# Spreading the linear attention's norm factors over the rows: one fp32 product per head, or two fp32r products of a high and a low part

## The reference, cut to what matters

```
o_g = gla_chunked(q_g, k_g, v_g, log_a)                 # (1, 512 rows, 4 heads, 128)
o_g = rms_norm(o_g, gla_out_norm[i]).reshape(B, S, GLA_WIDTH) * jax.nn.silu(g_r)
...
h = h + jnp.concatenate([o_g, o_m], axis=-1) @ w_out[i]

def rms_norm(x, g):
    y = x * lax.rsqrt(jnp.mean(x * x, axis=-1, keepdims=True) + EPS)
    return y * g
```

## Time and profile before

| | |
|---|---|
| median of the runs | 1650.19 us |
| profiled execution, its own time | 1649.77 us |
| its span (first to last instruction) | 1648.0 us |
| TensorE busy with products | 1639.9 us |
| VectorE busy | 938.9 us |
| ScalarE busy | 615.4 us |
| GpSimd busy | 84.5 us |
| mean granted TensorE clock | 0.999 of full |

### The profile page before, as it was taken

The page is one execution under the profiler, slowest core; times in us unless marked ns, Lnnn a source line. Parts: engine busy times, 40 slices in busy tenths (PEclk is TensorE's granted clock), DMA queues, the critical chain, the costliest instruction groups (busy, mean ns, idle before and its releaser), DMA issues.

```text
span 1648.0 us, 19096 instructions
## 1 busy us (share of the span) xinstructions
PE 1639.9 (100%) x8084; PEld 1336.8 (81%) x8084; DVE 938.9 (57%) x1384; ACT 615.4 (37%) x828; POOL 84.5 (5%) x80
## 2 busy tenths in 40 slices
PE   9999999999999999999999999999999999999999
PEld 7877878888888888888888888877777888888887
DVE  6797675444343546577466457545655577366353
ACT  5576433332222336433223223455555333122121
POOL 1300000000000000000000000311201100000000
PEclk9999999999999999999999999999999999999999
DMA  5300227444453421222322222322221233222311
GB/s 195 116 26 27 103 77 131 132 87 110 100 119 83 123 103 52 77 103 102 128 77 102 103 83 96 126 77 92 85 76 52 77 103 103 102 102 93 109 60 71
DMA packets 27910, 155.94 MB, mean 95 GB/s; under 512 B 3696, under 2 KB 5120, under 8 KB 11952
## 3 DMA queue, kind: packets, MB, share of 16 engines
q1 hardware_dynamic: 26352, 149.84, 25.4%
q0 software_dynamic: 1328, 4.86, 5.1%
q10 hardware_dynamic: 144, 0.00, 0.0%
HBM read 149.98 MB, written 4.72 MB: 94 GB/s over the span
## 4 chain that ended last, share of the span: by engine, by line
PE 96%; DVE 2%; ACT 1%; POOL 0%; DMA 0%; issue 0%; SPq 0%; DVEq 0%
PE bank L584 26%; PE bank L586 26%; PE bank L585 26%; PE bank L590 3%; PE bank L592 3%; PE bank L591 3%; PE bank L1215 1%; PE bank L1225 1%; PE bank L1241 1%; PE bank L839 1%; PE bank L824 1%; PE bank L1101 0%; PE bank L1203 0%; PE bank L768 0%; PE bank L606 0%; PE bank L864 0%
## 5 line engine op out<-in xcount | busy, mean ns | idle before, releaser
L584 PE MATMUL bank<-AH,WH 128*128 128x512 f32 (+1 forms) x1150 | 451.4, 393 | 1.5 <-DVE gsil L2007 1.4
L586 PE MATMUL bank<-AH,WL 128*128 128x512 f32 (+1 forms) x1150 | 447.8, 389 | 0.0
L585 PE MATMUL bank<-AL,WH 128*128 128x512 f32 (+1 forms) x1150 | 447.6, 389 | 0.0
L1674 DVE TENSOR_TENSOR WL<-RAW,WH 128x2048 fp32r<-128x2048 f32 (+1 forms) x133 | 298.5, 2247 | 189.9 <-ACT WH L1286 189.9
L1286 ACT ACTIVATE WH<-RAW 128x2048 fp32r<-128x2048 f32 (+1 forms) x133 | 248.3, 1871 | 258.9 <-PE bank L586 240.3
L584 PEld LDWEIGHTS bank<-AH,WH 128*128 128x128 f32 (+1 forms) x1150 | 215.5, 187 | 49.9 <-issue 2.6
L586 PEld LDWEIGHTS bank<-AH,WL 128*128 128x128 f32 (+1 forms) x1150 | 215.5, 187 | 46.0
L585 PEld LDWEIGHTS bank<-AL,WH 128*128 128x128 f32 (+1 forms) x1150 | 215.5, 187 | 45.3 <-issue 1.0
L584 PE MATMUL bank<-HH,WH 128*128 128x512 f32 x608 | 239.6, 394 | 0.0
L586 PE MATMUL bank<-HH,WL 128*128 128x512 f32 x608 | 238.4, 392 | 0.0
L585 PE MATMUL bank<-HL,WH 128*128 128x512 f32 x608 | 236.0, 388 | 0.0
(11 more groups left out here) (305 smaller groups left out, 1733.1 us busy)
## 6 DMA issues: line engine op xcount, KB each, us to landing
RAW<-in_W SPq DMA_DIRECT2D x124, 1024.0 KB, 4.8
RAW<-in_W SPq DMA_DIRECT2D x9, 768.0 KB, 4.2
X<-in_XT SPq DMA_DIRECT2D x16, 256.0 KB, 5.3
ev_scratch<-ev POOLq DMA_DIRECT2D x16, 160.0 KB, 7.7
Gb<-ev_scratch SPq DMA_DIRECT2D x16, 128.0 KB, 3.2
out<-X SPq DMA_DIRECT2D x8, 256.0 KB, 2.0
Gb<-ev_scratch SPq DMA_DIRECT2D x16, 112.0 KB, 2.7
RAW<-in_W SPq DMA_DIRECT2D x2, 512.0 KB, 5.2
```

What stands on the lines that cost most here:

```text
L584: e.matmul(o, a, h, start=first, stop=False)
L585: e.matmul(o, a, l, start=False, stop=False)
L586: return e.matmul(o, c, h, start=False, stop=last)
L1674: e.tensor_tensor(k.WL[j][:, 0:n], k.RAW[RAW_OF[u]][:, 0:n], k.WH[j][:, 0:n].bitcast(F), SUB).then_inc(*WLO.mark(u))
```

## The change

DVE first makes the table of a head into a high part rh of type fp32r (L2074 of the new kernel) and the rest rl (L2076), then two diagonals from them, diagH and diagL, both fp32r. TensorE multiplies an fp32r block of ones, `onesr`, by one and then the other into the same bank. diagH lies over dg or rb as before, diagL over sq[0] or sq[1]. As sq holds the squares until the last row sums are taken, and rh and rl have one buffer each, there are new waits: for the row sums of head 3, and for the diagonal of the head before. `onesr` is copied once near the program's start.

```
+    k.onesr, k.rh, k.rl = a.tile("onesr", [P, P], R), a.tile("rh", [P, 4], R), a.tile("rl", [P, 4])
+    k.diagH = [a.over(f"diagH{i}", [P, 4, P], at, R) for i, at in enumerate((dg_at, rb_at))]
+    k.diagL = [a.over(f"diagL{i}", [P, 4, P], sq_at + 4 * S * i, R) for i in range(2)]
...
     def spread_out(h):
         w.wait_ge(DVE("odiag", h), *free[4 + h % 2])
-        e.matmul(bank[4 + h % 2][:, :], ones, (k.acc, k.rb)[h % 2][:, :], start=True, stop=True).then_inc(*MM.mark("ospread", h))
+        b = bank[4 + h % 2]
+        e.matmul(b[:, :], k.onesr[:, :], k.diagH[h % 2][:, :, :], start=True, stop=False)
+        e.matmul(b[:, :], k.onesr[:, :], k.diagL[h % 2][:, :, :], start=False, stop=True).then_inc(*MM.mark("ospread", h))
         free[4 + h % 2] = [DVE("gained", h)]
...
     w.wait_ge(arrived(k, "cst"))
+    e.tensor_copy(k.onesr[:, :], cst[:, C_ONE:C_ONE + P])
     spread_rows(0)
...
     def out_diagonal(h):
         w.wait_ge(POOL("rg", h // 2))
         if h > 1:
             w.wait_ge(MM("ospread", h - 2))
-        r = k.rg[:, 4 * h:4 * h + 4]
-        d = (dg[:, :, :], rb[:, :].rearrange("p (q n) -> p q n", n=P))[h % 2]
-        e.tensor_tensor(d, ident[:, None, :].to_broadcast([P, 4, P]), r[:, :, None].to_broadcast([P, 4, P]), MUL).then_inc(
-            *DVE.mark("odiag", h))
+        r, eye = k.rg[:, 4 * h:4 * h + 4], ident[:, None, :].to_broadcast([P, 4, P])
+        if h:
+            w.wait_ge(DVE("odiag", h - 1))
+        e.tensor_copy(k.rh[:, :], r).then_inc(*DVE.mark("orh", h))
+        w.wait_ge(DVE("orh", h), MM("osum", 3))
+        e.tensor_tensor(k.rl[:, :], r, k.rh[:, :].bitcast(F), SUB).then_inc(*DVE.mark("orl", h))
+        e.tensor_tensor(k.diagH[h % 2][:, :, :], eye, k.rh[:, :].bitcast(F)[:, :, None].to_broadcast([P, 4, P]), MUL)
+        w.wait_ge(DVE("orl", h))
+        e.tensor_tensor(k.diagL[h % 2][:, :, :], eye, k.rl[:, :, None].to_broadcast([P, 4, P]), MUL).then_inc(*DVE.mark("odiag", h))
```

More of the change, by code:

```diff
@@ L188, in memory @@
     k.WL = [a.tile(f"WL{i}", [P, UE], R) for i in range(NW)]
+    rb_at = a.at
     k.rb = a.tile("rb", [P, S])
+    sq_at = a.at
     k.sq = [a.tile(f"sq{i}", [P, S]) for i in range(2)]
```

## The result

The new kernel takes 1659.22 us (median of four runs, 1657.82 to 1659.61), the kernel before 1650.28 on the same chip (four runs, 1648.57 to 1650.54). The ratio is 1.0058 [1.0045, 1.007]: 8.9 us slower. The forecast was 1650.9, with 1652.6 as the upper end of its range, so it was wrong, and on the side to which it had given 0.04. The profiled execution's own time is 1659.61 us and its span 1657.8.

What follows compares the result with a forecast made beforehand. TensorE was taken as the bound, VectorE as late in 200 to 220 us: its second pair's extra 2.0 us less slack outweighs TensorE's 1.6 us saving, +0.71 us on the 1650.19 median, giving 1650.9 us, range 1649.0 to 1652.6.

Steps and rivals of the forecast that it cites:

- the side to which it had given 0.04: Whole kernel: measurably slower, beyond 0.2% or 3.3 us, from a clock fall and more behind it; chance 0.04.
- The step that the prediction worked out: Second pair of heads, 200 to 220 us: VectorE's extra 2.0 us less its slack delays TensorE by +0.71 us.
- 1.60 us a head: VectorE, per head: cast, subtraction, diagH and diagL take 1.60 us where one diagonal took 0.60.
- the means where they were forecast: VectorE, after the first pair's diagonals: the means start at 206.65 instead of 203.77.
- the forecast 0.6 and 1.1: TensorE waits 0.6 us for head 2's diagonal and about 1.1 us for head 3's before their spreads.
- the wait for X: TensorE waits 0.8 us before the second half's second output block, which starts near 219.95.
- Rival 2: 200 to 220 us: VectorE's additions come early enough, TensorE's whole 1.6 us saving stays, 1648.6 us; chance 0.06.
- Rival 4: Spreads on TensorE: fp32r products take 0.43 us, no saving, total +0.8 us; counted within the forecast's 0.68.
- rival 1: VectorE's heads: waits on its own results are free, 1.36 us a head, +0.1 us, 1650.3 us; chance 0.13.
- Rival 3: 213 to 224 us: new waits bring a second clock fall, 1.5 us on top, +2.2, 1652.4 us; chance 0.13.
- From 219.95 all is shifted alike, if nothing else slips: Everything behind the second half's second output block keeps its pace, only shifted by 0.7 us, with no further loss.
- The copy to `onesr`: VectorE near the program's start: one 128x128 operation fits where it waited 1.23 us for POOL, costing nothing.

Runs made afterwards that it cites:

- e2_tail: The new kernel with onesr, rh and rl in free memory behind all other tiles, which stand at their old places: 1650.9 us, ratio 1.0006.
- e1: The kernel before with 576 unused bytes behind m4, so later tiles move as in the new kernel, no instruction changed: 1657.01 us, ratio 1.0042.
- e3: The kernel before with 192 unused bytes behind m4: 1644.87 us, ratio 0.9969.
- e6: The kernel before with 320 unused bytes behind m4: 1656.96 us, ratio 1.0042.
- e7: The kernel before with 128 unused bytes behind m4: 1657.71 us, ratio 1.0047.
- e11: The kernel before with 224 unused bytes behind m4: 1657.43 us, ratio 1.0046.
- e12: The kernel before with 704 unused bytes behind m4: 1645.04 us, ratio 0.9973.
- e10_after_pad128: The new kernel with 128 unused bytes of padding: 1645.9 us, ratio 0.9979.
- e9_best: The new kernel with rh and rl made once for two heads, diagL formed by ScalarE, and 64 bytes of padding: 1643.49 us, ratio 0.9966.
- e4_pad448: The kernel before with 448 unused bytes behind m4: 1643.52 us, ratio 0.9961.
- e5_all64: The kernel before with every tile moved by 64 bytes: 1650.17 us, ratio 0.9998.
- e8_w64: The kernel before with weights WH and WL moved 64 bytes, activations AH, AL, HH and HL unmoved modulo 256: 1667.26 us, ratio 1.0103.

## Why the prediction was wrong

**What held.** The step that the prediction worked out was right in place and size: products of 0.23 us, 1.60 us a head, the means where they were forecast (207.51 less the older shift of 0.78 is 206.73, for 206.65), waits of 0.57 and 0.87 for the forecast 0.6 and 1.1, the wait for X (0.58, forecast 0.8), VectorE as the bound of the stretch. It cost +0.79 in the profiles and +0.95 by e2_tail's median, for a forecast of +0.71. Rival 2 (the saving stays) fell with the waits. Its slack of 1.1 us on VectorE was counted from three of the idle times in brackets; by the starts, twelve operations of 0.60 in the 8.98 us from 209.52 to 218.50 leave 1.8. The sum of +0.71 went by starts and isn't touched by that. Rival 4 (products of 0.43) fell with the spacing. The waits on VectorE's own results aren't free, so rival 1 fell too: in the new kernel diagL runs from 205.31 to the start of its waiter at 206.03, 0.72 us, and diagH, without a waiter, from 204.71 to 205.31, 0.60. The rule of the Trainium skill, "VectorE: DVE Perf Modes", "The DRAIN you can't avoid", by which the semaphore adds nothing, doesn't agree with that.

Rival 3 (a second fall of the clock) didn't come either. Two windows of the new kernel, the first as the earlier trace rows, the second over the new waits:

```profile
194.70:201.90 7.20, 7.20 (x30) 5.93 (x30) 3.88 (x5) 3.19 (x4) 1.64 (x1) 0.76 0.08 9
209.00:222.00 13.00, 10.98 (x45) 8.03 (x45) 11.65 (x20) 2.46 (x4) 0.39 (x1) 1.00 0.06 10
```

The granted clock there is 1.00.

**What failed.** The step "From 219.95 all is shifted alike, if nothing else slips". The prediction asked of the rest of the program only whether anything arrives late. The diff had one more effect, visible in its first line: three tiles declared ahead of HH and HL. It put the moving operand of 1824 products, a quarter of TensorE's time, from distance 64 to 128, at 4.3 ns each: 425.3 - 417.4 = 7.9 us, a term that the prediction had at nothing. The products with OH and OL, which also lie behind the three tiles, rise from about 229.5 to 233 ns, 173 distances, +0.6 us. Together 8.5 where the profiles show 8.27 behind the first HH product. The copy to `onesr` was priced as an instruction, at nothing, and the 576 bytes weren't priced at all. The form of the error is that the cost of TensorE's product was taken as one number for one shape, while the earlier trace rows already mixed operands: those eleven products, of 0.232, aren't of HH.

The Trainium skill's page "SBUF — State Buffer", section "Operand start alignment", would not have warned: it lets an fp32 operand start at any multiple of 4 bytes, and says itself that this is about legality and that nothing was timed. In these runs all places are legal and their times differ by 24 us.

**What stays open.** 0.78 us of the profiles' difference arises ahead of attended 4. Most of it is at the start, where the first product of L584 stands at 6.92 before and of L590 at 7.37 now, behind a transfer of X that landed at 5.79:

```profile
1.66 4.13 DMA X<-in_XT
...
7.37 0.45 PE bank L590
```

Before, the chain began with a weight transfer that landed at 4.70. No run ties it to the change: the kernels with the instructions of before and fast AH products (e1, e3 to e7, e11 and e12) reach attended 0 anywhere from 180.10 to 180.64 us, before at 179.99, the new kernel at 180.79, e2_tail and e10_after_pad128 at 180.67, and e9_best, which has the copy to `onesr` as well, at 180.15. Most of the 0.78 us can be the scatter of single executions; the rest stays open. Nor is it shown why the distance matters, why 256 is its period (0 and 256 modulo 512 were alike, and so were the two places of 128, by 320 and by 576; no shorter period fits 0, 32, 64, 128 and 192), or why 64 lies between and 32 doesn't. Which read of the weights counts, that of the same product or that of the next one's, can't be told, as all weights stand at one place modulo 256. Not shown either: whether it holds for products whose weights aren't loaded anew each time. All of these load them.

## What to carry to other kernels

A tile added to a memory plan is an edit to every instruction whose operands lie behind it: put new tiles last, or compare the places of all hot operands before and after. In a stream of fp32r products of 128x512 with a weight load each, keep the moving operand and the stationary one at the same place modulo 256 bytes; in this kernel one line of padding was worth 5.1 us (e4_pad448, 1643.53 against 1648.59 among executions at a granted clock of 1.000; the medians' 6.4 has luck with the clock in it), and the change that was meant to speed it up cost some 0.8 us with the places held. And when TensorE's busy time rises with an unchanged count and no idle time, compare the mean ns of its groups by operand before looking for waits.

## What the runs showed of the hardware

- In a stream of fp32r products of 128x512, the mean distance between starts is 226.7 ns where the moving operand stands 0 bytes behind the stationary one modulo 256, 229.0 ns at 64, and 233.3 ns at 32, 128 and 192; only these five were measured.
- Both operands moved together by 64 bytes cost nothing (e5_all64, 1650.17 against 1649.91 us), and which of the two is moved makes no difference (e8_w64).
- On VectorE, a 128x512 operation whose follower waits for its result takes 0.72 us from start to start, one without such a wait 0.60 (new kernel, 205.31 to 206.03 and 204.71 to 205.31).
- The clock's fall behind the narrow products comes in some profiled executions only, and it explains part of the scatter. Two windows over the same stretch, e4_pad448 without it:

```profile
192.00:206.00 14.00, 14.00 (x93) 12.24 (x92) 6.94 (x10) 5.57 (x6) 3.28 (x2) 1.00 0.23 76
```

and e12_pad704, the same instructions, with it:

```profile
192.00:206.00 14.00, 14.00 (x89) 12.17 (x88) 6.34 (x9) 5.20 (x6) 3.27 (x2) 0.88 0.22 76
```

From attended 2 to attended 4 are 7.31 us in e4_pad448 and 8.89 in e12_pad704: 1.6 us for this fall, most of the 1.8 between their spans (1641.4 and 1643.2). In e10_after_pad128 it is longer, and the same way takes 10.14. Of the fourteen profiled executions it shows in before, the change, e1, e2, e5, e10 and e12. What decides whether it comes wasn't studied. This is why differences under 2 us were read from stretches of the profile, and not from medians.
